# Query and scores of x's first 128 tokens in two halves of 64, all heads of the first 64 ahead

## The chip, the cores and the metric

One NeuronCore of a Trainium2 chip. It has five engines with queues of their own: TensorE (PE: matmuls, and PEld for its weight loads), VectorE (DVE), ScalarE (ACT), GpSimd (POOL) and SyncE (SP), and 16 DMA engines that move data between HBM and SBUF. The metric is the device time in microseconds, the median of three runs.

## The reference

Two blocks run one after the other on 256 tokens of width 1024, in float32. The first is a plain block (attention, a gated branch, a feed-forward of four times the width). The second has two layers; each mixes x with a context of 256 tokens and then sends every token through a table of experts. The part that matters here is that last step, cut from the reference:

```
def peer_ffn(h, w_query, sub_keys, u_tab, v_tab):        # h: 128 tokens at a time
    q = (hc @ w_query).reshape(PEER_CHUNK, PEER_HEADS, 2, D_KEY // 2)
    s = jnp.einsum('chpd,hpnd->chpn', q, sub_keys).astype(jnp.float32)
    s_top, i_top = lax.top_k(s, PEER_TOPK)
    cand = s_top[:, :, 0, :, None] + s_top[:, :, 1, None, :]
    best, pos = lax.top_k(cand.reshape(...), PEER_TOPK)
    eid = jnp.take_along_axis(cand_id, pos, axis=-1)
    gate = jax.nn.softmax(best, axis=-1).astype(hc.dtype)
    u = jnp.take(u_tab, eid, axis=0)
    act = jax.nn.gelu(jnp.einsum('chkd,cd->chk', u, hc)) * gate
    v = jnp.take(v_tab, eid, axis=0)
    return jnp.einsum('chk,chkd->cd', act, v)
```

There are 8 heads, 128 keys in each half of a head's query, and 16 best of 128 and then of the pairs. Every token so reads 128 rows of u_tab and 128 rows of v_tab, 4 KB each. In the second layer only x goes on to the output.

## The kernel before

The kernel is written as one hand-ordered program for each engine; every engine has its own copy of the same walk over the stages (mixer, routing, experts), and semaphores tie them together. Tokens are in tiles of 128: tiles 0 and 1 are the context in layer 0, 2 and 3 are x in layer 0, 4 and 5 are x in layer 1. "c0", "x0", "c1", "x1" name a layer's mixer, and `route_first` and `route_second` route its two tiles.

Routing of a tile. TensorE makes the query with `query` (L902): for each u of 0 and 1, four blocks of 128 rows (four heads), each a sum over 8 pieces of H, with weights W as the stationary side and the tile's 128 token columns as the moving side. ScalarE copies the bank to QP. `scores` (L912) multiplies QP with the keys, and ScalarE copies the banks to the tile sc. VectorE then takes `steps_of(n)`: "top" steps (`sixteen_best`, four rows of 128 scores each), "pairs" steps, and four "keys" steps. ScalarE helps twice in `routes`: at "pairs 0" it spreads the ranks (tixe, semaphore ranks_spread), and at "keys 0" it takes the exponent (best_exp). At the end TensorE transposes the expert numbers and gates (L948, L953), VectorE writes idxT and raises idx_ready (L1718 to L1721), and GpSimd may gather.

Tiles 2 and 4 (SPLIT) are routed in two parts of 64 tokens. In a part, partition 64b + t holds token t with the heads of group b, so that 64 tokens of eight heads fill 128 partitions. The first part is `routes(n, 0)` in `route_first`; the second is routed in `route_second`, beside the second tile's branch products. `query` and `scores` of such a tile are done for all 128 tokens, heads 0 to 3 first (u = 0) and heads 4 to 7 then (u = 1); the scores are written by 64 tokens (L927).

The expert stream. A visit is the work for one pair of tokens: TensorE spreads the hidden rows (L468), VectorE takes the dot with the gathered rows of u (L1174), ScalarE the gelu, and TensorE later sums the rows of v (L482). GpSimd issues four indirect DMAs for a pair (L2448, L2458), at most three pairs ahead. Visits are dealt into the rest of the program by `beat(key, us)`: each call adds its weight in us to a debt, and each 6.8 (PACE) of debt places a visit, in TensorE's program and in the same place of the others', as long as pairs are routed. Before c1 the first stream (tiles 0 to 3) is closed, and the second stream (tiles 4 and 5) is opened after `route_first("x1")`, so nothing is visited while tile 4's first part is routed. In x0 the stream of the context's tiles runs on.

What stands behind the scores in `route_first` of x0 and x1: the transposes of the hidden rows (`hidden`, L885), a gate product of the tile's second half (`merge_unit(tag, 1, "z", 0)`, L669), the routing steps with a second gate product at "pairs 0", and the transposes of the indices. Weights come in chunks of up to 2 MB through a ring of three slots; SyncE asks for the next chunk when `done_with_weights` tells that a slot's chunk has been used.

## Time and profile before

| what | us |
|---|---|
| median of three runs | 3284.21 |
| the three runs | 3279.72, 3284.21, 3287.22 |
| the profiled execution, its own time | 3281.02 |
| its span, first to last instruction | 3279.3 |
| PE busy, matmuls (share of the span) | 2348.2 (72%) |
| PE weight loads | 1356.8 (41%) |
| DVE busy | 1692.5 (52%) |
| ACT busy | 577.9 (18%) |
| POOL busy | 1481.8 (45%) |
| moved by DMA | 1097.74 MB, mean 335 GB/s |

The span is shorter than the profiled execution's time by 1.7 us, which lie around it. A busy share is a mean over stages with different limits; where one engine waits for another is read from the single instructions. The trace holds two records for one float32 matmul of the program, and as many weight loads. The page gives the granted clock of TensorE in tenths of full speed, the windows as a fraction: 1.00 is 2.4 GHz and 0.50 is 1.2 GHz.

### The profile page before, as it was taken

The numbers are of one execution on the slowest core, as the hardware profiler recorded it, in microseconds if no ns is written. First come the engines' busy times: TensorE is split into PE (matmuls) and PEld (weight loads), VectorE is DVE, ScalarE is ACT, GpSimd is POOL, SyncE is SP. The second block draws the span as 40 slices with busy tenths as digits, with TensorE's granted clock in tenths as the row PEclk, the third lists the DMA queues.
The fourth block names the chain that finished last, engine by engine and source line by source line (L and its number), as shares of the span: only waits on it lengthen the run. The fifth ranks groups of instructions, "written<-read, shape, count | busy, mean of one in ns | idle before, by whom it ended". The sixth has DMA issues, their size and how long they took to land.

```text
span 3279.3 us, 40034 instructions
## 1 busy us (share of the span) xinstructions
PE 2348.2 (72%) x13944; PEld 1356.8 (41%) x13944; DVE 1692.5 (52%) x4471; ACT 577.9 (18%) x1213; POOL 1481.8 (45%) x1577
## 2 busy tenths in 40 slices
PE   6899957899899888885775754445997765544444
PEld 5477724466676554762540300002587452100000
DVE  2521576554333577347559554443724647744444
ACT  2320231411100235111111400001331111100000
POOL 1100035444444444434547577773000556777775
PEclk9999978799999897996875755556898886555555
DMA  8958579899999986997999999995245999999998
GB/s 310 356 185 297 204 265 349 318 355 361 368 364 370 349 320 240 372 398 282 402 395 397 350 403 409 409 409 215 73 161 199 366 402 360 393 409 409 409 409 348
DMA packets 351015, 1097.74 MB, mean 335 GB/s; under 512 B 27936, under 2 KB 39264, under 8 KB 350816
## 3 DMA queue, kind: packets, MB, share of 16 engines
q0 software_dynamic: 240192, 880.90, 69.9%
q1 hardware_dynamic: 110624, 214.29, 18.2%
q8 instruction: 112, 1.84, 0.2%
q14 instruction: 87, 0.71, 0.1%
HBM read 1094.03 MB, written 1.05 MB: 334 GB/s over the span
## 4 chain that ended last, share of the span: by engine, by line
PE 44%; DVE 18%; DMA 14%; issue 12%; PEld 6%; ACT 3%; POOL 1%; PEldq 1%; DVEq 0%; ACTq 0%; POOLq 0%
PE ps L446 18%; PE ps L482 11%; DVE UV L1174 8%; DMA UV<-in_v_tab,idxT 8%; PE ps L468 4%; PE ps L669 3%; PEld ps L669 3%; DMA W<-in_w_out 3%; PEld ps L446 3%; ACT arena L1894 2%; PE ps L438 2%; DMA W<-in_w_mod 2%; DMA W<-in_w_in 1%; PE ps L613 1%; PE ps L571 1%
## 5 line engine op out<-in xcount | busy, mean ns | idle before, releaser
L1174 DVE SCALAR_TENSOR_TENSOR UV<-ps,UV 128x1024 f32<-128x1024 f32 x768 | 909.8, 1222 | 816.3 <-PE ps L468 798.6
L2448 POOL DMA_INDIRECT UV<-in_u_tab,idxT x768 | 723.8, 942 | 1156.5 <-DVE UV L1174 613.3
L482 PE MATMUL ps<-UV,acts 128*32 128x512 f32 x3072 | 607.1, 873 | 486.5 <-DVE acts L1183 341.2
L2458 POOL DMA_INDIRECT UV<-in_v_tab,idxT x768 | 725.6, 945 | 266.7 <-issue 200.9
L446 PE MATMUL ps<-H,W 128*128 128x256 f32 (+2 forms) x2528 | 503.2, 361 | 32.4 <-ACT H L1894 25.9
L446 PEld LDWEIGHTS ps<-H,W 128*128 128x128 f32 (+1 forms) x2528 | 435.3, 199 | 117.6 <-issue 66.2
L468 PE MATMUL ps<-hs,selb 32*128 32x512 bf16 x1536 | 203.1, 515 | 200.8 <-DVE UV L1174 194.3
L482 PEld LDWEIGHTS ps<-UV,acts 128*32 128x32 f32 x3072 | 76.4, 127 | 634.9 <-DVE acts L1183 436.1
L468 PEld LDWEIGHTS ps<-hs,selb 32*128 32x128 bf16 x1536 | 42.0, 96 | 595.5 <-issue 329.1
L1894 ACT ACTIVATE gel<-dots 128x2 f32<-128x2 f32 x384 | 77.2, 202 | 1152.9 <-DVE UV L1174 1141.4
L446 PE MATMUL ps<-arena,W 128*128 128x256 f32 (+1 forms) x1120 | 254.3, 384 | 11.8 <-issue 4.8
L1894 ACT ACTIVATE arena<-ps 128x512 f32<-128x512 f32 (+6 forms) x260 | 138.9, 539 | 678.1 <-PE ps L446 461.0
L446 PEld LDWEIGHTS ps<-arena,W 128*128 128x128 f32 (+1 forms) x1120 | 208.2, 189 | 68.0 <-issue 36.4
L669 PEld LDWEIGHTS ps<-H,W 128*128 128x128 f32 x1536 | 184.2, 202 | 25.3 <-issue 17.1
L669 PE MATMUL ps<-H,W 128*128 128x128 f32 x1536 | 187.7, 286 | 8.7 <-DMA W<-in_w_in 6.9
L2424 POOL DMA_DIRECT2D UV<-in_w_mod x18 | 16.1, 900 | 234.3 <-ACTq L1946 201.1
L1894 ACT ACT_TABLE_LOAD x85 | 109.1, 1283 | 54.2 <-PE ps L613 24.6
L669 PE MATMUL ps<-arena,W 128*128 128x128 f32 x640 | 84.2, 297 | 16.5 <-DMA W<-in_w_out 10.1
L669 PEld LDWEIGHTS ps<-arena,W 128*128 128x128 f32 x640 | 81.4, 211 | 24.0 <-issue 15.6
L571 PE MATMUL ps<-UV,gateT 128*32 128x512 f32 x432 | 71.4, 632 | 19.0 <-DMA W<-in_w_mod 9.4
L1462 DVE SCALAR_TENSOR_TENSOR arena<-arena,vec 128x256 f32<-128x256 f32 x180 | 79.3, 483 | 4.8 <-DVE arena L1155 0.7
L1183 DVE TENSOR_TENSOR acts<-gel,gateT 128x2 f32<-128x2 f32 x384 | 61.4, 160 | 10.4 <-ACT gel L1894 9.7
(228 smaller groups left out, 1948.5 us busy)
## 6 DMA issues: line engine op xcount, KB each, us to landing
W<-in_w_in SPq DMA_DIRECT2D x42, 2048.0 KB, 14.3
UV<-in_w_mod POOLq DMA_DIRECT2D x18, 2048.0 KB, 12.4
W<-in_w_ff SPq DMA_DIRECT2D x16, 2048.0 KB, 14.2
W<-in_w_out SPq DMA_DIRECT2D x12, 2048.0 KB, 13.9
W<-in_w_query SPq DMA_DIRECT2D x10, 2048.0 KB, 19.5
UV<-in_w_ada POOLq DMA_DIRECT2D x9, 2048.0 KB, 11.8
W<-in_w_mod POOLq DMA_DIRECT2D x6, 2048.0 KB, 20.1
UV<-in_u_tab,idxT POOLq DMA_INDIRECT x768, 8.1
```

The costliest lines, as they stand in the source:

```text
L438: last = mm(o, lhs[k], rhs[k], start=(k == 0), stop=(k == n - 1))
L446: last = mm(o, w[:, k, col:col + m], src[:, k, c], start=(k == 0), stop=(k == kt - 1))
L468: last = mm(ps[:, HB + r, :], selb[q, u:u + 1].to_broadcast([32, P]), hs[q, n % 2, s, :], start=True, stop=True)
L482: last = mm(ps[q:q + GROUP, YB, :], acts[:, tok % SLOTS, GROUP - 1 - r:2 * GROUP - 1 - r], Vs[:, tok % SLOTS, hf * 512:(hf + 1) * 512], st ...
L571: last = mm(o[q:q + 32, :], cond32[:, 4 * kh + kk, :], w[j][:, 4 * kh + kk, :], start=(kk == 0), stop=(kk == 3))
L669: last = mm(o[:, e * P:(e + 1) * P], w[:, k, e * P:(e + 1) * P], src[:, k, :], start=(k == 0), stop=(k == kt - 1))
L1174: dve.scalar_tensor_tensor(out=Us[:, j, :], in0=ps[:, b:b + 2, :].rearrange("p a b -> p (a b)"), scalar=1.0, in1=Us[:, j, :], op0=MUL, op1 ...
L1183: dve.tensor_tensor(out=acts[:, j:j + 2, GROUP - 1], in0=gel[:, j:j + 2], in1=gateT[:, n % 2, t:t + 2], op=MUL).then_inc(sem("acts"), 1)
L1462: last = dve.scalar_tensor_tensor(out=a, in0=u, scalar=wt, in1=a, op0=MUL, op1=ADD)
L1894: return act.activation(o, i, f, **kw)
L2448: pool.indirect_dma_start(Us[:, j, :], None, A["u_tab"], off).then_inc(sem(f"u_arrived{j}"), 16)
L2458: pool.indirect_dma_start(Vs[:, j, :], None, A["v_tab"], off).then_inc(sem(f"v_arrived{j}"), 16)
```

## The change

For x's first tile of each layer (tiles 2 and 4), query and scores go through four steps instead of two. The order is: first 64 tokens with heads 0 to 3, first 64 tokens with heads 4 to 7, then the same for the other 64 tokens. The new functions `query_half` and `scores_half` stand in TensorE's and ScalarE's programs; the weights of both u are kept in the ring until the second half has used them. Two branches of `scores` for a tile of two parts are gone. The waits count by `queries_before(n)`, and VectorE's first "top" steps wait for the scores of their own 64 tokens. The debt of the beats is 4.0 for each of the four query steps, 16 in all, where two queries and two score steps had 18. The context's first tile is untouched.

```diff
+            def query_half(tag, n, u, r, first=False):
+
+                w = weights(("wq", tag, n % 2, u))
+                o, at = bank(("wq", n, u, r)), n % 2 * P + HALF * r
+                for e in range(4):
+                    last = feature(o[:, e * HALF:(e + 1) * HALF], w, e * P, H, DT, first=first and e == 0, c=slice(at, at + HALF))
+                full(last, ("wq", n, u, r))
+                if r:
+                    done_with_weights()
+
+            def scores_half(n, u, r):
+
+                pe.wait_ge(sem("query_ready"), queries_before(n) + 2 * r + u + 1)
+                o = [bank(("sc", n, u, r, p)) for p in range(2)]
+                for i in range(2):
+                    for b in range(2):
+                        h, at = 4 * u + 2 * b + i, HALF * r
+                        for p in range(2):
+                            last = mm(o[p][HALF * b:HALF * b + HALF, i * P:(i + 1) * P], QP[n % 2][64 * p:64 * p + 64, h, at:at + HALF],
+                                      keys[64 * p:64 * p + 64, h, :], start=True, stop=True)
+                            if (i, b) == (1, 1):
+                                full(last, ("sc", n, u, r, p))
...
                 n = TILE_OF[tag]
-                for u in range(2):
+                for u in range(2 if tag == "c0" else 0):
                     query(tag, n, u, first=(u == 0))
                     beat(("wq", n, u), 7.0)
                     if u == 0:
                         pe.wait_ge(sem("keys_loaded"), nxt("keys_loaded", 16))
                     scores(n, u)
+                for i in range(4 if tag != "c0" else 0):
+                    r, u = i // 2, i % 2
+                    query_half(tag, n, u, r, first=(i == 0))
+                    beat(("wq", n, u, r), 4.0)
+                    if i == 0:
+                        pe.wait_ge(sem("keys_loaded"), nxt("keys_loaded", 16))
+                    scores_half(n, u, r)
...
-                    dve.wait_ge(sem("scores_ready"), 4 * n + 2 * (e // 2 + 1 if parts(n) == 1 else e + 1))
+                    dve.wait_ge(sem("scores_ready"), 2 * queries_before(n) + 2 * (e // 2 + 1 if parts(n) == 1 else 2 * r + e + 1))
...
+            def query_half(n, u, r):
+
+                p = full_bank(act, ("wq", n, u, r))
+                link(A_(QP[n % 2][:, 4 * u:4 * u + 4, HALF * r:HALF * r + HALF], p[:, 0:4 * HALF].rearrange("p (e t) -> p e t", e=4)))
+                act.sem_inc(free(("wq", n, u, r)), 1)
+                act.sem_inc(sem("query_ready"), 1)
+                beat("wq", n, u, r)
+
+            def scores_half(n, u, r):
+
+                for q in range(2):
+                    p = full_bank(act, ("sc", n, u, r, q))
+                    link(A_(s4[:, r, 2 * u:2 * u + 2, q, :], p[:, 0:2 * P].rearrange("p (h k) -> p h k", h=2)))
+                    act.sem_inc(free(("sc", n, u, r, q)), 1)
+                    act.sem_inc(sem("scores_ready"), 1)
```

TensorE in layer 1, `route_first("x1")`, before. L446 is the query (here one row for 32 matmuls, 128 columns moving), L927 the scores, L885 the transposes of the hidden rows, L669 the two gate products, L953 and L954 the transposes of the indices:

```order
L446 MATMUL ps<-H,W 128x128 x32
L927 MATMUL ps<-arena 64x128 x16
L446 MATMUL ps<-H,W 128x128 x32
L927 MATMUL ps<-arena 64x128 x16
L885 MATMUL ps<-ident,H 128x128 x8
L669 MATMUL ps<-H,W 128x128 x64
L953 MATMUL ps<-ident,arena 64x64
```

The same place in the changed kernel, where L450 is the query, L924 the scores, L889, L673 and L972 the rest:

```order
L450 MATMUL ps<-H,W 128x64 x32
L924 MATMUL ps<-arena 64x128 x8
L450 MATMUL ps<-H,W 128x64 x32
L924 MATMUL ps<-arena 64x128 x8
L450 MATMUL ps<-H,W 128x64 x32
L924 MATMUL ps<-arena 64x128 x8
L450 MATMUL ps<-H,W 128x64 x32
L924 MATMUL ps<-arena 64x128 x8
L889 MATMUL ps<-ident,H 128x128 x8
L673 MATMUL ps<-H,W 128x128 x64
L972 MATMUL ps<-ident,arena 64x64
```

Two groups of 32 query matmuls have become four, all ahead of the transposes and the gate products.

ScalarE at the same place, before, from the first query copy to the exponent. The row that waits for `ranked` is the spread of the ranks:

```order
L1894 ACTIVATE arena<-ps 128x512 [waits psum_full,idx_ready]
L1894 ACTIVATE arena<-ps 128x2x2x128 [waits act_chain,psum_full] x2
L1894 ACTIVATE arena<-ps 128x512 [waits act_chain,psum_full]
L1894 ACTIVATE arena<-ps 128x2x2x128 [waits act_chain,psum_full] x2
L1894 ACTIVATE arena<-ps 128x512 [waits act_chain,psum_full]
L1894 ACTIVATE arena<-ps 128x512 [waits psum_full]
L1894 ACT_TABLE_LOAD [waits psum_full]
L1894 ACTIVATE VC<-ps 128x512 [waits gates_used]
L1894 ACTIVATE arena<-arena 128x2048 [waits act_chain,ranked]
```

And in the changed kernel:

```order
L1922 ACTIVATE arena<-ps 128x4x64 [waits psum_full,idx_ready]
L1922 ACTIVATE arena<-ps 128x2x128 [waits act_chain,psum_full] x2
L1922 ACTIVATE arena<-ps 128x4x64 [waits act_chain,psum_full]
L1922 ACTIVATE arena<-ps 128x2x128 [waits act_chain,psum_full] x2
L1922 ACTIVATE arena<-ps 128x4x64 [waits act_chain,psum_full]
L1922 ACTIVATE arena<-ps 128x2x128 [waits act_chain,psum_full] x2
L1922 ACTIVATE arena<-ps 128x4x64 [waits act_chain,psum_full]
L1922 ACTIVATE arena<-ps 128x2x128 [waits act_chain,psum_full] x2
L1922 ACTIVATE arena<-ps 128x512 [waits act_chain,psum_full]
L1922 ACTIVATE arena<-ps 128x512 [waits psum_full]
L1922 ACT_TABLE_LOAD [waits psum_full]
L1922 ACTIVATE VC<-ps 128x512 [waits gates_used]
```

The copies of the second 64 tokens now stand ahead of the gate product's copy (VC) and of the spread behind it, whose row reads as before.

TensorE in layer 0, `route_first("x0")`, of the changed kernel, from the first query step to the gate product. A pair of rows L472 and L486 is a visit:

```order
L450 MATMUL ps<-H,W 128x64 x32
L924 MATMUL ps<-arena 64x128 x8
L450 MATMUL ps<-H,W 128x64 x32
L472 MATMUL ps<-hs,selb 128x512 x4
L486 MATMUL ps<-UV,acts 32x512 x4
L924 MATMUL ps<-arena 64x128 x8
L450 MATMUL ps<-H,W 128x64 x32
L472 MATMUL ps<-hs,selb 128x512 x4
L486 MATMUL ps<-UV,acts 32x512 x4
L924 MATMUL ps<-arena 64x128 x8
L450 MATMUL ps<-H,W 128x64 x32
L924 MATMUL ps<-arena 64x128 x8
```

Two visits stand between the four query steps and a third behind the transposes that follow; before there were also three up to the gate product, one behind each query and one behind the transposes.

## Rows read from the trace of the kernel before

**Rows 1.** Windows: stretch, its length, busy us, granted clock, DMA share, GB/s.

```profile
core 0: us, PE busy (x) PEld busy (x) DVE busy (x) ACT busy (x) POOL busy (x), PEclk, DMA share, GB/s
...
1490.00:1520.00 30.00, 13.99 (x100) 10.27 (x104) 25.80 (x112) 6.54 (x7) 6.87 (x7) 0.67 0.40 143
...
2252.00:2541.00 289.00, 240.51 (x1612) 197.72 (x1608) 130.59 (x365) 83.63 (x150) 1.87 (x2) 0.91 0.38 129
...
2550.00:2710.00 160.00, 118.05 (x936) 83.71 (x938) 86.40 (x235) 23.05 (x50) 81.18 (x86) 0.83 1.02 393
...
2860.00:3240.00 380.00, 184.94 (x892) 26.64 (x892) 183.19 (x384) 16.03 (x76) 278.10 (x298) 0.50 1.03 409
...
1520.00:1780.00 260.00, 170.79 (x1248) 99.53 (x1240) 168.54 (x552) 37.73 (x80) 146.84 (x156) 0.74 1.02 393
```

**Rows 2.** Timeline of GpSimd: start, us, instruction, count [idle before <- releaser].

```profile
1513.38 0.94 POOL L2448 DMA_INDIRECT UV<-in_u_tab,idxT  x1 [21.61 <-DVEq L1721]
...
2541.64 0.94 POOL L2448 DMA_INDIRECT UV<-in_u_tab,idxT  x1 [286.48 <-DVEq L1721]
```

**Rows 3.** Timeline of TensorE's matmuls in layer 1, `route_first("x1")`.

```profile
2495.10 10.20 PE L446 MATMUL ps<-H,W 128*128 128x128 f32 x64 [3.98 <-ACT H L1894]
...
2506.20 1.10 PE L927 MATMUL ps<-arena 64*64 64x128 f32 x32 [0.91 <-ACTq L2240]
2507.23 7.41 PE L446 MATMUL ps<-H,W 128*128 128x128 f32 x64
2515.45 1.10 PE L927 MATMUL ps<-arena 64*64 64x128 f32 x32 [0.80 <-ACTq L2240]
...
2517.41 7.31 PE L669 MATMUL ps<-H,W 128*128 128x128 f32 x64
2524.98 7.38 PE L669 MATMUL ps<-H,W 128*128 128x128 f32 x64 [0.26 <-issue]
2539.54 0.49 PE L953 MATMUL ps<-ident,arena 64*64 64x64 f32 x4 [7.18 <-DVEq L1708]
```

**Rows 4.** Timeline there of VectorE (top 1, keys 0) and ScalarE (the spread).

```profile
2518.20 0.88 DVE L1612 MAX8 arena<-arena 128x8 f32<-128x128 f32 x4 [4.02 <-ACTq L2252]
...
2526.88 1.91 ACT L1894 ACTIVATE arena<-arena 128x2048 bf16<-128x2048 bf16 x1 [0.18 <-ACT VC L1894]
...
2532.97 0.69 DVE L1630 TENSOR_TENSOR arena<-arena,iotax 128x1024 bf16<-128x1024 bf16 x1
```

**Rows 5.** Timeline of TensorE and VectorE in layer 0, `route_first("x0")`.

```profile
1438.62 9.31 PE L446 MATMUL ps<-H,W 128*128 128x128 f32 x64 [2.54 <-ACT H L1894]
...
1458.07 0.40 PE L468 MATMUL ps<-hs,selb 32*128 32x512 bf16 x4
1458.39 1.07 PE L482 MATMUL ps<-UV,acts 128*32 128x512 f32 x8
...
1470.67 0.40 PE L468 MATMUL ps<-hs,selb 32*128 32x512 bf16 x4
...
1473.55 0.87 DVE L1612 MAX8 arena<-arena 128x8 f32<-128x128 f32 x4
...
1481.88 1.94 PE L482 MATMUL ps<-UV,acts 128*32 128x512 f32 x8
```

**Rows 6.** Records by line: ns min/median/max, first and last start; one timeline row.

```profile
L446 PE MATMUL ps<-H,W x29: 274/276/276, 2501.8 to 2504.9; 128*128 128x128 f32 x29
L446 PEld LDWEIGHTS ps<-H,W x28: 191/192/193, 2501.9 to 2504.9; 128*128 128x128 f32 x28
...
L446 PE MATMUL ps<-H,W x23: 420/422/422, 2495.7 to 2500.3; 128*128 128x128 f32 x23
L446 PEld LDWEIGHTS ps<-H,W x22: 333/333/334, 2495.9 to 2500.4; 128*128 128x128 f32 x22
...
2346.99 0.97 PEld L825 LDWEIGHTS ps<-onecol,arena 96*128 96x128 f32 x8 [0.53 <-issue]
```

**Rows 7.** Windows: stretch, its length, busy us, granted clock, DMA share, GB/s.

```profile
2352.00:2366.00 14.00, 14.00 (x25) 6.27 (x25) 11.99 (x22) 0.93 (x2) 0.00 (x0) 0.50 0.01 1
2491.00:2501.00 10.00, 6.02 (x29) 5.93 (x29) 3.55 (x9) 3.49 (x9) 0.00 (x0) 0.50 0.35 135
```

More of the change, by code:

```diff
@@ L46, in part_no, with queries_before @@
     return sum(parts(m) for m in range(n)) + r
+def queries_before(n):
+    return sum(2 * parts(m) for m in range(n))
 def steps_of(n):
@@ L912, in scores @@
             def scores(n, a):
-                pe.wait_ge(sem("query_ready"), 4 * (n // 2) + 2 * (n % 2) + a + 1)
+                pe.wait_ge(sem("query_ready"), queries_before(n) + a + 1)
                 o = [bank(("sc", n, a, p)) for p in range(2)]
-                for hh in range(4 if parts(n) == 1 else 0):
+                for hh in range(4):
                     h = 4 * a + hh
@@ L922, in scores @@
                             full(last, ("sc", n, a, p))
-                for i in range(4 if parts(n) == 2 else 0):
-                    for b in range(2):
-                        h, at = 4 * a + 2 * b + i % 2, i // 2 * HALF
-                        for p in range(2):
-                            last = mm(o[p][HALF * b:HALF * b + HALF, i * P:(i + 1) * P], QP[n % 2][64 * p:64 * p + 64, h, at:at + HALF],
-                                      keys[64 * p:64 * p + 64, h, :], start=True, stop=True)
-                            if (i, b) == (3, 1):
-                                full(last, ("sc", n, a, p))
                 beat(("sc", n, a), 2.0)
@@ L1736, in route_first @@
                 n = TILE_OF[tag]
-                for u in range(2):
+                for u in range(2 if tag == "c0" else 0):
                     beat("wq", n, u)
                     beat("sc", n, u)
+                for i in range(4 if tag != "c0" else 0):
+                    beat("wq", n, i % 2, i // 2)
                 for u in range(2 if tag == "c0" else 0):
@@ L2246, in scores @@
                     p = full_bank(act, ("sc", n, a, q))
-                    if parts(n) == 1:
-                        link(A_(w4[:, 4 * a:4 * a + 4, q, :], p.rearrange("p (a b) -> p a b", b=P)))
-                    else:
-                        link(A_(s4[:, :, 2 * a:2 * a + 2, q, :], p.rearrange("p (r h k) -> p r h k", r=2, h=2)))
+                    link(A_(w4[:, 4 * a:4 * a + 4, q, :], p.rearrange("p (a b) -> p a b", b=P)))
                     act.sem_inc(free(("sc", n, a, q)), 1)
@@ L2277, in route_first @@
                     act.wait_ge(sem("idx_ready"), part_no(n, 0))
-                for u in range(2):
+                for u in range(2 if tag == "c0" else 0):
                     query(n, u)
                     scores(n, u)
+                for i in range(4 if tag != "c0" else 0):
+                    query_half(n, i % 2, i // 2)
+                    scores_half(n, i % 2, i // 2)
                 mods_at(tag, "queried")
```

## Prediction

> **What bounds the kernel now.** I read the busy shares and DMA of chosen stretches first, then the waits of the GpSimd queue, then single instructions around the two places that the change touches. Over each of the long stretches 1520 to 1780, 2550 to 2710 and 2860 to 3240 us the DMA engines are full (share 1.02, 1.02, 1.03) [rows 1]. They carry the gathers of expert rows, four indirect DMAs for a pair of tokens. So the end comes a fixed amount of traffic after the moment at which gathers may begin, as long as nothing later starves them. Twice they have nothing to do. In 1490 to 1520 the share is 0.40, and in 2252 to 2541 it is 0.38 [rows 1]. Both holes end when the indices of x's first 64 tokens come out of routing: at 1513.38 after 21.61 us of waiting and at 2541.64 after 286.48 us the first gather of such a half is issued, released by VectorE at L1721 [rows 2]. I call these moments G0 (layer 0) and G1 (layer 1). A microsecond later at either is a microsecond later at the end, and both add up: the hardware works in program order behind them, on full DMA.
>
> What sets G1 [rows 3, 4]: TensorE makes query 0 at 2495.10, its scores at 2506.20, query 1 at 2507.23, scores at 2515.45, some transposes, then two gate products at 2517.41 and 2524.98. VectorE starts the second "top" step at 2518.20, having waited for the scores. It works without a stop to the "keys" step at 2532.97, and the transposes of the indices follow at 2539.54, for which TensorE had waited 7.18 us. ScalarE's spread of the ranks (2526.88, 1.91 us, done at 2528.8), which the keys step needs, stands behind ScalarE's copy of the first gate product. It has 4.2 us to spare.
>
> What sets G0 [rows 5]: here experts of the context's tokens are worked on in between. TensorE starts query 0 at 1438.62; after queries, scores, transposes, three such visits and the first gate product comes the visit at 1470.67, 32.05 us later. VectorE has that visit ahead of its first top step, which begins at 1473.55. There is no slack: what TensorE does before 1470.67 is on the path.
>
> **What the change removes and adds.** Two passes over the query weights for 128 tokens become four for 64. Each pass still has 32 matmuls, which the trace shows as 64 records, and 64 loads of 128x128 weights; only the moving side falls from 128 to 64 columns. The sum thus hangs on the price of a record with 64 columns, which the trace doesn't have. From both sides: with 128 columns at the high clock 29 records start from 2501.8 to 2504.9, 111 ns apart. With one moving column, eight loads of 128 columns take 0.97 us; less the last one's 0.19 that is 111 ns apart as well [rows 6]. One column costs as much as 128, so the load sets the pace and 64 columns lie between equal ends: 7.4 us for a half pass, as for a whole one (2507.23). At the low clock 23 records of 128 columns start from 2495.7 to 2500.3, 209 ns apart. The load's own duration grows there from 192 to 333 ns, the matmul's from 276 to 422, by nearly the same amount [rows 6]. I take it that loads go slower with the clock and price a half pass at 64 x 0.209 = 13.4 us.
>
> The Trainium skill, TensorE: Matmul & The Clock Gate, section LDWEIGHTS, gives a load as its columns over 1.2, so about 107 ns, with no word of the clock. By it a half pass at the low clock would be 6.8 us and the whole sum would be that of the second case below. The rows [rows 6] speak against it: 333 ns against 192.
>
> **Which clock.** Both first passes begin after TensorE has been idle for some microseconds. In 2491 to 2501 the granted clock is 0.50, the 1.2 GHz level [rows 7], and it rose during the first whole pass, which streams its columns without a gap. A half pass has loads that take as long and half the columns. The nearest stretches are 2860 to 3240, busy about half the time, at 0.50 for 380 us [rows 1], and 2352 to 2366, busy 14.00 of 14.00 us with narrow weights, also at 0.50 [rows 7]. I take the low level to last through all four half passes of layer 1. In layer 0 the visits and scores between the passes are dense work, which may lift it midway.
>
> Layer 1 at the low clock: four passes 53.5; each followed by a wait for the copy (0.9) and a score group of half size (0.5, at the low clock 1.0), 7.6 together; the transposes 1.9; the gate product 7.3 and 1.0 for the part of it still slow. From 2495.1 that ends at 2566.4 instead of 2524.7, 41.7 later. Less the spread's 4.2: G1 **+37.5**. At the high clock: passes 10.2 + 3 x 7.4 = 32.4, then 4 x 1.4, 1.0 and 7.3, 16.7 later, G1 +12.5.
>
> Layer 0: at the high clock passes 9.3 + 3 x 7.4 = 31.5, three visits of 1.4 (1458.07 to 1459.46) [rows 5], score groups 2.0, two waits of 0.9 that no visit covers, transposes 1.0, the gate product 7.4: 47.9 instead of 32.05, G0 +15.9. At the low clock throughout: 53.5 + 3 x 2.5 (the low clock's 1.94 [rows 5] and twice 0.32 ahead of it) + 4.0 + 1.8 + 2.0 + 8.2 = 77, G0 +45. Between the ends I take **+30**, the level rising at the visit after the second or third pass.
>
> Side costs at nothing: the first half's scores come a little earlier, but the spread or the visit ends later, so VectorE waits. The weight ring gives query 0's slot back after the third pass instead of the first. The weights of the second gate product are then asked for 22 us or more before they are needed at the low clock, and about 18 at the high one; SyncE's queue otherwise keeps its order. ScalarE's eight score copies are half as wide as the four before. Should that cover fail, one 2 MB chunk costs up to the 14.3 us in which such chunks land (median of the page). From G0 and G1 on, the order is the old one.
>
> Sum: 37.5 + 30 = 67.5 us. The profiled execution took 3281.0, so 3348.5; the median of the three runs is 3284.2, 3.2 above it, so **3352**.
>
> **Rivals.**
> Second case, the clock is high in nearly all passes, or loads don't slow with it: +12.5 and +15.9 = 28.4, 3312.6. For it: before, the first pass of layer 0 took 9.31 us against 10.20 in layer 1 [rows 3, 5], so less of it ran at the low level. Against it: a half pass streams columns half of the time.
>
> Third case, the other side: columns, not loads, price a record, 0.056 us, so a half pass is 3.6 us and the first one, paced by ScalarE, some 6.6, together 17.4. Layer 0: 17.4 + 4.2 + 2.0 + 1.8 + 1.0 + 7.4 = 33.8, G0 +1.8. Layer 1: the first gate product ends 1.7 later, the spread at 2530.5, which is 2.4 ahead of the old keys step, and VectorE, with its scores by 2510, is there before: G1 -2.4. Together -0.6, 3283.6, not slower. It decides below 4.5 us for a half pass, 70 ns a record. The eight one-column records [rows 6] speak against it. The Trainium skill, TensorE: Matmul & The Clock Gate, section Back-to-back issue gap, gives 1 to 64 columns some 60 cycles and 128 columns 134, which is this case.
>
> Fourth, the delay is partly taken up later: between G0 and the end of the first stream a stretch with the DMA not quite full could catch up some microseconds. That moves the first two cases down by up to 8 us and is in the range.
>
> **How the numbers follow.** Low clock for most of the half passes 0.70 (layer 0 from +16 to +45, so 3334 to 3370 as its own range), second case 0.17, third 0.08, something else 0.05. A measurement tells 0.2%, 6.6 us, from no change. The first two cases are slower, with a little of the rest: slower 0.90, same 0.07, faster 0.03. The range must reach into the second case: 3306 (3312.6 less 6 caught up) to 3370 (+82.5 and the spread of the runs, 3).
>
> **What would show it.** Records with 64 columns 111 ns apart at the high and about 209 at the low clock; a granted clock of 0.50 from the first half pass of layer 1 to the gate product; the first gather of that half at 2541.6 + G0's shift + 37; the keys step released by ScalarE's spread; a longer hole in the DMA at both places and the same full DMA behind. Records 56 to 70 ns apart would make it wrong, and so would an end that moves less than the two first gathers.

## The result and the profile after

The changed kernel takes 3357.64 us, the median of six runs (3345.56 to 3365.09); the kernel before, measured beside it, 3282.76 (3273.68 to 3289.12). The ratio is 1.0231, with a 95% interval of 1.0211 to 1.0251: slower by 2.3%. The forecast was 3352 with a range of 3306 to 3370. The profiled execution is the shortest of the six, 3345.56 us; what probably makes the others longer comes below, with x0_only.

The head of the page of the changed kernel:

```profile
span 3343.8 us, 40590 instructions
...
PE 2418.5 (72%) x14200; PEld 1418.9 (42%) x14200; DVE 1692.1 (51%) x4471; ACT 580.0 (17%) x1225; POOL 1486.5 (44%) x1577
```

TensorE has 70 us more of busy time and the span is 64.5 longer; VectorE, ScalarE and GpSimd have nearly the busy time that they had. The first gathers of the two first halves, from the timeline of GpSimd (start, us, instruction, idle time before and what ended it), answer to [rows 2]:

```profile
1540.28 0.94 POOL L2492 DMA_INDIRECT UV<-in_u_tab,idxT  x1 [22.81 <-DVEq L1747]
...
2606.64 0.94 POOL L2492 DMA_INDIRECT UV<-in_u_tab,idxT  x1 [325.98 <-DVEq L1747]
```

They moved from 1513.38 to 1540.28 and from 2541.64 to 2606.64, by 26.9 and 65.0 us, the second including the first. The end moved by 64.5. From here on I call the time from a layer's first query record to this gather its **stretch**. Before, the stretches were 74.76 us in layer 0 (from 1438.62) and 46.54 in layer 1 (from 2495.10); now they are 102.94 and 85.59, that is 28.18 and 39.05 more. Between the first gather and the next layer's first record lie 980.8 us (981.7 before), behind the second gather 737.2 (737.7): hardly a microsecond was given back.

TensorE's matmuls in layer 1, the same columns as [rows 3] (L450 is the query, L924 the scores, L889 the transposes of hidden rows, L673 the gate products, L972 the transposes of the indices):

```profile
2521.05 13.89 PE L450 MATMUL ps<-H,W 128*128 128x64 f32 x64 [3.98 <-ACT H L1922]
2535.64 1.13 PE L924 MATMUL ps<-arena 64*64 64x128 f32 x16 [0.69 <-issue]
2536.70 13.91 PE L450 MATMUL ps<-H,W 128*128 128x64 f32 x64
...
2552.26 13.91 PE L450 MATMUL ps<-H,W 128*128 128x64 f32 x64
...
2567.83 13.91 PE L450 MATMUL ps<-H,W 128*128 128x64 f32 x64
...
2585.16 8.88 PE L673 MATMUL ps<-H,W 128*128 128x128 f32 x64
2594.30 7.38 PE L673 MATMUL ps<-H,W 128*128 128x128 f32 x64 [0.26 <-issue]
2604.79 0.34 PE L972 MATMUL ps<-ident,arena 64*64 64x64 f32 x4 [3.11 <-DVEq L1734]
```

Four half passes of 13.9 us stand where two whole ones of 10.20 and 7.41 stood. Windows of the changed kernel (stretch, length, busy us, granted clock, DMA share, GB/s, as in [rows 1, 7]):

```profile
2536.70:2550.60 13.90, 13.90 (x68) 13.72 (x64) 5.17 (x32) 0.77 (x2) 0.00 (x0) 0.50 0.01 1
...
2567.80:2581.80 14.00, 13.94 (x68) 13.72 (x64) 0.46 (x2) 0.79 (x3) 0.00 (x0) 0.50 0.39 145
...
2252.00:2606.00 354.00, 293.77 (x1792) 238.41 (x1792) 142.50 (x390) 85.82 (x161) 16.82 (x18) 0.81 0.38 135
...
2925.00:3305.00 380.00, 185.10 (x896) 26.39 (x888) 183.00 (x382) 15.81 (x75) 279.55 (x298) 0.50 1.03 409
```

The half passes ran at 0.50, the 1.2 GHz level, until the gate product. The window of the hole in the DMA, 2252 to the first gather, has the same share of 0.38 as the 289 us before, but here it takes in the last gathers of the first stream (16.82 us of GpSimd instead of 1.87). The hole itself grew by 39.5 us, which is what GpSimd's wait for the indices grew by (325.98 instead of 286.48). The last stream behind it is as full as before (1.03).

What held VectorE, and ScalarE's spread of the ranks, as in [rows 4]:

```profile
2553.56 0.87 DVE L1638 MAX8 arena<-arena 128x8 f32<-128x128 f32 x4 [10.34 <-ACTq L2285]
...
2598.22 0.69 DVE L1656 TENSOR_TENSOR arena<-arena,iotax 128x1024 bf16<-128x1024 bf16 x1 [29.93 <-ACT arena L1922]
...
2596.20 1.91 ACT L1922 ACTIVATE arena<-arena 128x2048 bf16<-128x2048 bf16 x1 [0.18 <-ACT VC L1922]
```

VectorE had the scores of the first 64 tokens at 2553.5, was through with the top and pairs steps at 2568.3, and then waited 29.93 us for the spread, which stands on ScalarE behind the copy of the gate product, which stands on TensorE behind the two half passes of the other 64 tokens. Being first ahead of the others brought VectorE nothing.

Layer 0, as in [rows 5] (L472 and L486 are a visit):

```profile
1437.34 13.70 PE L450 MATMUL ps<-H,W 128*128 128x64 f32 x64 [2.55 <-ACT H L1922]
...
1452.79 13.91 PE L450 MATMUL ps<-H,W 128*128 128x64 f32 x64
1466.64 0.61 PE L472 MATMUL ps<-hs,selb 32*128 32x512 bf16 x4
1467.18 1.88 PE L486 MATMUL ps<-UV,acts 128*32 128x512 f32 x8
1468.99 0.67 PE L924 MATMUL ps<-arena 64*64 64x128 f32 x16
1469.59 7.36 PE L450 MATMUL ps<-H,W 128*128 128x64 f32 x64
...
1478.98 7.36 PE L450 MATMUL ps<-H,W 128*128 128x64 f32 x64
...
1497.56 0.40 PE L472 MATMUL ps<-hs,selb 32*128 32x512 bf16 x4
```

Two half passes at the low clock, 13.70 and 13.91 us, and from the visit between the second and the third on two at the high one, 7.36 each. The visit behind the gate product came 60.22 us after the first record instead of 32.05; from it to the gather it took 42.7 us in both kernels.

### The profile page after: what moved, and what is told of

Same layout as the page of the kernel before. It is cut to its first block, busy times and chain, and to the rows that moved or that the text cites. A ratio compares the mean times of both kernels' runs of the same rounds, so it can differ in the third digit from the quotient of the medians.

```text
span 3343.8 us, 40590 instructions
## 1 busy us (share of the span) xinstructions
PE 2418.5 (72%) x14200; PEld 1418.9 (42%) x14200; DVE 1692.1 (51%) x4471; ACT 580.0 (17%) x1225; POOL 1486.5 (44%) x1577
## 3 DMA queue, kind: packets, MB, share of 16 engines
q8 instruction: 114, 1.87, 0.2%
## 4 chain that ended last, share of the span: by engine, by line
PE 46%; DVE 17%; DMA 13%; issue 12%; PEld 6%; ACT 3%; POOL 2%; PEldq 1%; DVEq 0%; ACTq 0%; POOLq 0%
PE ps L450 19%; PE ps L486 11%; DMA UV<-in_v_tab,idxT 8%; DVE UV L1200 7%; PE ps L673 4%; PE ps L472 3%; PEld ps L450 3%; PEld ps L673 2%; ACT arena L1922 2%; PE ps L442 2%; DMA W<-in_w_mod 2%; DMA W<-in_w_in 1%; DMA W<-in_w_out 1%; PE ps L575 1%; PE ps L617 1%
## 5 line engine op out<-in xcount | busy, mean ns | idle before, releaser
L486 PE MATMUL ps<-UV,acts 128*32 128x512 f32 x3072 | 610.4, 878 | 487.6 <-DVE acts L1209 349.1
L450 PE MATMUL ps<-H,W 128*128 128x256 f32 (+3 forms) x2784 | 564.3, 369 | 31.9 <-ACT H L1922 25.1
L450 PEld LDWEIGHTS ps<-H,W 128*128 128x128 f32 (+1 forms) x2784 | 495.4, 214 | 118.2 <-issue 66.4
L472 PE MATMUL ps<-hs,selb 32*128 32x512 bf16 x1536 | 203.1, 515 | 203.1 <-DVE UV L1200 197.0
L486 PEld LDWEIGHTS ps<-UV,acts 128*32 128x32 f32 x3072 | 76.5, 127 | 636.6 <-DVE acts L1209 442.8
L472 PEld LDWEIGHTS ps<-hs,selb 32*128 32x128 bf16 x1536 | 41.7, 96 | 597.8 <-issue 329.1
L450 PE MATMUL ps<-arena,W 128*128 128x256 f32 (+1 forms) x1120 | 254.3, 384 | 11.7 <-issue 4.7
L450 PEld LDWEIGHTS ps<-arena,W 128*128 128x128 f32 (+1 forms) x1120 | 207.7, 189 | 68.3 <-issue 36.3
L673 PEld LDWEIGHTS ps<-H,W 128*128 128x128 f32 x1536 | 188.3, 205 | 22.4 <-issue 16.3
L673 PE MATMUL ps<-H,W 128*128 128x128 f32 x1536 | 191.8, 289 | 5.8 <-DMA W<-in_w_in 4.2
L2468 POOL DMA_DIRECT2D UV<-in_w_mod x18 | 16.1, 900 | 235.1 <-ACTq L1974 201.2
L673 PE MATMUL ps<-arena,W 128*128 128x128 f32 x640 | 82.6, 293 | 13.0 <-DMA W<-in_w_out 6.9
L673 PEld LDWEIGHTS ps<-arena,W 128*128 128x128 f32 x640 | 79.8, 207 | 20.3 <-issue 16.8
```

The lines of the kernel that those rows point to most:

```text
L450: last = mm(o, w[:, k, col:col + m], src[:, k, c], start=(k == 0), stop=(k == kt - 1))
L472: last = mm(ps[:, HB + r, :], selb[q, u:u + 1].to_broadcast([32, P]), hs[q, n % 2, s, :], start=True, stop=True)
L486: last = mm(ps[q:q + GROUP, YB, :], acts[:, tok % SLOTS, GROUP - 1 - r:2 * GROUP - 1 - r], Vs[:, tok % SLOTS, hf * 512:(hf + 1) * 512], st ...
L673: last = mm(o[:, e * P:(e + 1) * P], w[:, k, e * P:(e + 1) * P], src[:, k, :], start=(k == 0), stop=(k == kt - 1))
```

## The experiments

The kernel before was timed beside each group of experiments: 3280.1 us beside x1_only to wide_moving, 3281.0 beside warm to spread_first, 3279.3 beside warm14 and narrow_load, 3280.2 beside the last two. The stretches are first record to first gather, each from one profiled execution; passes are those of layer 1.

| kernel | layer 0 stretch | layer 1 stretch | query passes, layer 1 | median us | ratio to before, 95% interval |
|---|---|---|---|---|---|
| before | 74.76 | 46.54 | 10.20, 7.41 | 3282.8 | 1 |
| the change | 102.94 | 85.59 | 13.89, 3 x 13.91 | 3357.6 | 1.0211 to 1.0251 |
| x1_only | 74.91 | 84.74 | 13.74, 3 x 13.91 | 3319.3 | 1.0097 to 1.0132 |
| x0_only | 119.68 | 46.54 | 10.20, 7.41 | 3319.0 | 1.0082 to 1.0129 |
| umajor | 119.91 | 84.93 | 13.70, 3 x 13.91 | 3363.2 | 1.0219 to 1.0270 |
| wide_moving | 90.85 | 58.15 | 10.21, 3 x 7.41 | 3310.8 | 1.0068 to 1.0106 |
| warm | 103.25 | 84.15 | 12.88, 3 x 13.91 | 3339.1 | 1.0153 to 1.0189 |
| before_warm | 73.86 | 44.89 | 8.54, 7.41 | 3278.1 | 0.9983 to 1.0004 |
| late | 74.70 | 61.79 | 13.88, 13.91, 7.26, 7.36 | 3302.8 | 1.0053 to 1.0084 |
| spread_first | 103.28 | 83.68 | 13.70, 3 x 13.91 | 3352.4, one run | none |
| warm14 | 88.43 | 55.27 | 7.25, 3 x 7.36 | 3305.5 | 1.0058 to 1.0100 |
| narrow_load | 87.71 | 54.70 | 9.73, 6.42, 6.43, 6.42 | 3302.0 | 1.0056 to 1.0097 |
| before_split | 82.42 | 53.87 | 13.41, 11.53 | 3297.6 | 1.0033 to 1.0063 |
| late_narrow | 74.47 | 45.02 | 10.50, 6.43, 6.43, 6.42 | 3286.6 | 1.0010 to 1.0028 |

In warm, before_warm and warm14 the stretch begins with the first real query record, behind the extra matmuls.

### One layer alone: x1_only and x0_only

Both keep the two functions of the change for one tile and give the other the whole passes back:

```diff
+HALVED = (4,)          # x0_only: (2,)
 def queries_before(n):
-    return sum(2 * parts(m) for m in range(n))
+    return sum(4 if m in HALVED else 2 for m in range(n))
...
-                for i in range(4 if tag != "c0" else 0):
+                for i in range(4 if n in HALVED else 0):
```

> Only layer 1 (tile 4) goes in four half passes; layer 0 (tile 2) has its two whole passes back. My theory: the two places are independent and add up, each delaying its own first gather. In the traces the stretch from the first query to the first gather grew by 39.05 us in layer 1 (46.54 to 85.59) and by 28.18 in layer 0 (74.76 to 102.94). Expected here: 46.5 + 39 = 85.6 us in layer 1, 74.8 in layer 0, and a time of 3282.8 + 39 = 3322 us (3318 to 3326). Rival, a delay in layer 0 is partly caught up later and layer 1 costs more than its own share: over 3330.

> Only layer 0 (tile 2) goes in four half passes; layer 1 is as before. Theory (independent, additive): from the first query to the first gather 102.9 us in layer 0 and 46.5 in layer 1, time 3282.8 + 28 = 3311 us (3306 to 3315). Rival, the stream of layer 0 has room and takes part of the delay up before the mixer of layer 1: below 3304.

Layer 1 came as expected: 3319.3 us, 39.2 above the kernel before, runs within 2 us of each other (3318.0 to 3319.7). The two medians add up to 78.1, near the 74.9 of the change. Layer 0 did not come as expected: 38.9 above instead of 28, and the runs lie from 3310.2 to 3326.9. The windows of TensorE in layer 0 of x0_only, at the second half pass, the visit behind it and the third half pass, and below them those of the changed kernel, tell why:

```profile
1456.30:1470.20 13.90, 13.90 (x72) 13.78 (x68) 0.00 (x0) 0.77 (x2) 0.00 (x0) 0.50 0.01 1
1470.20:1473.60 3.40, 3.40 (x29) 0.99 (x28) 2.45 (x5) 0.59 (x2) 0.67 (x1) 0.50 0.00 0
1473.60:1487.60 14.00, 13.94 (x68) 13.73 (x64) 0.00 (x0) 0.79 (x3) 3.07 (x4) 0.50 0.44 150
```

```profile
1452.80:1466.60 13.80, 13.80 (x68) 13.72 (x64) 0.00 (x0) 0.77 (x2) 0.00 (x0) 0.50 0.00 1
1466.60:1469.60 3.00, 3.00 (x30) 0.75 (x29) 2.23 (x3) 0.59 (x2) 0.19 (x1) 0.62 0.00 0
1469.60:1477.00 7.40, 7.35 (x68) 7.21 (x64) 0.22 (x3) 0.78 (x3) 3.56 (x4) 1.00 0.73 247
```

The instructions are the same, and the clock rose in one execution and not in the other. So layer 0 has two outcomes from one execution to the next: about 103 us (the change, warm, spread_first) where it rises midway, and about 120 (x0_only, umajor) where it stays low through all four. That is two values of one stretch over five profiles. x0_only's own profile is of its longest run, 3326.9, 46.8 above the kernel before, and its shortest, 3310.2, is 30.1 above it: about the delays of the one and of the other outcome. The times alone don't prove it, since the kernel before also spreads by 8 to 15 us, and of the change itself only the shortest run has a profile.

### The order: umajor

```diff
-                    r, u = i // 2, i % 2
+                    u, r = i // 2, i % 2
```

(and the waits and ScalarE's copies to match)

> All four half passes stay, at the same place, but in the order of before: heads 0 to 3 for the first and then the second 64 tokens, then heads 4 to 7. Theory: the cost lies in the number and the clock of the passes, not in whose scores come first, because VectorE waits for the spread behind all four. Expected: the same as the changed kernel, 3357.6 us within 4, both stretches within 2 us of 85.6 and 102.9. Rival, the order itself costs (VectorE's early first steps or the ring slots held longer): nearer to the kernel before, below 3340.

Measured 3363.2 us, a little more than the 3357.6 expected and far from 3340. The layer-1 stretch is 84.93: whose scores come first doesn't matter, four passes do. Layer 0 took its long outcome in this profile (119.91 instead of 102.9), which is the miss of this expectation.

### Twice the columns: wide_moving

```diff
-    last = feature(o[:, e * HALF:(e + 1) * HALF], w, e * P, H, DT, first=first and e == 0, c=slice(at, at + HALF))
+    last = feature(o[:, e * P:(e + 1) * P], w, e * P, H, DT, first=first and e == 0, c=in_h(n))
```

> The changed kernel, but each of the four passes streams all 128 token columns, and ScalarE copies the 64 that the step wants; the other 64 are computed and dropped, so TensorE has twice the columns to do. Theory: a record is paced by its weight load, and the half pass is slow because the low clock lasts; with 128 columns the clock rises in the first pass and each later pass takes 7.4 us. Expected: passes 10.2, 7.4, 7.4, 7.4 in layer 1, granted clock 1.00 after the first, the layer-1 stretch 46.5 + 12.5 = 59 us, the layer-0 one 74.8 + 16 = 91, time 3282.8 + 28.4 = 3311 us (3305 to 3318), 46 faster than the changed kernel. Rival, columns or the traffic of the passes set the price: as slow as the changed kernel or slower, 3358 or more.

The passes of layer 1 in the timeline of TensorE:

```profile
2510.03 10.21 PE L450 MATMUL ps<-H,W 128*128 128x128 f32 x64 [3.98 <-ACT H L1922]
...
2521.53 7.41 PE L450 MATMUL ps<-H,W 128*128 128x128 f32 x64
```

Twice the columns, 47 us faster: 3310.8, the two stretches 16.1 and 11.6 above the kernel before, where the prediction's second case had 15.9 and 12.5. So the change costs some 28 us by its additional passes even at the high clock (31 by the medians), and the rest, 44 to 47, by the low one.

### What lowers the clock: warm and warm14

```diff
                 o, at = bank(("wq", n, u, r)), n % 2 * P + HALF * r
+                for _ in range(6 if first else 0):          # warm14: 14
+                    mm(o[:, 0:SEQ], ones[:, :], wide(dftc[:, :, :]), start=True, stop=True)
```

> The changed kernel with six extra matmuls (ones times a constant table, 128x128 by 256 columns, result overwritten) on TensorE ahead of the first half pass of both layers, where it waits 2.5 and 4.0 us for H. Theory: the half passes are slow because they begin at the low clock and cannot raise it; once it is high they keep it, as the last two of layer 0 did (1.00, 7.36 us each). Expected: four passes of 7.4 us at a granted clock of 1.00 in both layers, stretches from the first record to the first gather of 59 us in layer 1 and 91 in layer 0 plus 1 to 2 for the extra work, time 3282 + 30 + 3 = 3315 us (3310 to 3322). Rival, 64 columns cannot hold the high level without visits in between: only the first pass or two gain, 3335 to 3350.

Measured 3339.1, within the rival's numbers, and my theory in this form fell. (The two stretches of the profile are only 1.1 us shorter in sum than those of the change, while the medians are 18.5 apart. Where these come from is not shown; more runs with the short outcome of layer 0 are a possibility.) Windows around the start of the first half pass of layer 1 (2521.24):

```profile
2520.00:2521.00 1.00, 0.00 (x0) 0.00 (x0) 0.97 (x4) 0.30 (x1) 0.00 (x0) 1.00 0.78 283
2521.00:2522.00 1.00, 0.76 (x4) 0.59 (x4) 0.61 (x2) 1.00 (x4) 0.00 (x0) 1.00 0.00 0
...
2524.00:2525.00 1.00, 1.00 (x9) 1.00 (x9) 0.00 (x0) 0.00 (x0) 0.00 (x0) 0.90 0.00 0
2525.00:2526.00 1.00, 1.00 (x6) 1.00 (x6) 0.00 (x0) 0.00 (x0) 0.00 (x0) 0.50 0.00 0
```

The pass began at the high clock and lost it within 4 us. That leaves two readings: half passes lose the level by themselves, or the start does, where TensorE first waits 1.30 us for H and then 15 records take 3.02 us because ScalarE delivers H piece by piece.

> As warm, with 14 extra matmuls instead of six. With six the granted clock was 1.00 when the first half pass of layer 1 began (2521.24) and fell to 0.50 at about 2524.9, after a wait of 1.30 us for H and 15 records in 3.02 us, each waiting for ScalarE's pieces of H. Theory: not the half passes themselves lose the level but their ragged start; in late the level held through two half passes in a row (7.26 and 7.36 us). Fourteen take about 6.4 us (12 records took 2.76), so that all pieces of H are there when the pass begins, some 2.6 us later than before. Expected: four passes of 7.4 us in both layers, granted clock 1.00, the first gather 58 to 60 us after H came in layer 1 and about 91 to 93 in layer 0, time 3281 + 30 = 3311 us (3306 to 3318). Rival, half passes lose the level sooner or later by themselves: 3325 to 3345.

```profile
2509.75 7.25 PE L450 MATMUL ps<-H,W 128*128 128x64 f32 x64
...
2526.84 7.36 PE L450 MATMUL ps<-H,W 128*128 128x64 f32 x64
2535.39 7.36 PE L450 MATMUL ps<-H,W 128*128 128x64 f32 x64
...
2539.00:2543.00 4.00, 3.75 (x34) 3.61 (x33) 3.41 (x18) 0.21 (x1) 0.00 (x0) 1.00 0.63 238
```

Half passes don't lose the level by themselves. With a gap-free start all four ran at 1.00 in both layers (the last row is the end of the fourth), for 33 us in layer 1, and the kernel takes 3305.5, 52 less than the change, for 28 additional matmuls whose products nobody reads. These delay the first real record by 1.9 us in layer 1 and 3.5 in layer 0, which the stretches of the table leave out; from ScalarE's first piece of H the first gather comes after 57.8 and 92.6 us, as expected. The 14 matmuls do two things at once, they take the wait away and keep TensorE at work longer ahead of the pass, and no run separates the two. So half passes held the level over this time, but from the low one they did not win it back in layer 1 of the change, and the low clock is some 50 of the 75 us.

### The clock in the kernel before: before_warm

The same six matmuls ahead of its first whole pass of tiles 2 and 4.

> The kernel before with the same six extra matmuls ahead of the first whole query pass of tiles 2 and 4. Theory: whole passes raise the clock by themselves after some 5 us, so there is only 10.20 - 7.41 = 2.8 us to win in layer 1 and 9.31 - 7.41 = 1.9 in layer 0, less what the extra work overhangs (about 1 each): 3280.1 - 3 = 3277 us, 0.1%, within what can be told. Rival, the extra work delays more than it gives: 3283 or more.

```profile
2489.39 8.54 PE L446 MATMUL ps<-H,W 128*128 128x128 f32 x64 [1.30 <-ACT H L1896]
...
2494.00:2496.00 2.00, 2.00 (x21) 2.00 (x20) 0.00 (x0) 0.00 (x0) 0.00 (x0) 1.00 0.03 8
```

This adds to the reading of warm: behind the same six matmuls, the same wait of 1.30 us for H and the same pieces of H from ScalarE, a whole pass kept the level (the row is from its middle), where the half pass had fallen to 0.50. In layer 0 it was the same, 8.37 against 11.85 us. So the start alone doesn't lose the level; in warm it was such a start together with 64 moving columns behind 128-column loads.

The interval of the ratio, 0.9983 to 1.0004, includes no change. In the profile the passes took 8.54 instead of 10.20 in layer 1 and 8.37 instead of 9.31 in layer 0; the stretches are 1.65 and 0.90 shorter. It is the best version of this study by its median, and not one that the measurement separates from the kernel before.

### What stands behind: spread_first and late

In spread_first ScalarE spreads the ranks ahead of its copy of gate product 0, in layer 1:

```diff
                 if tag != "c0":
+                    if n == 4:
+                        spread_ranks(PH // 2, part_no(n, 0) + 1, 0)
                     merge_unit(tag, 1, "z", 0)
```

> The changed kernel, but in layer 1 ScalarE spreads the ranks ahead of its copy of gate product 0. Theory: VectorE's keys step then starts some 10 us earlier (it had waited 29.93 us for the spread), but the transposes of the indices stand on TensorE behind both gate products, which end 80.6 us after the first query record. So only the 3.1 us go that TensorE had waited there: the layer-1 stretch falls from 85.6 to 82.5 us. Rival, the spread alone was the path: 75.5 us. (Layer 0 is untouched; only the layer-1 stretch is read.)

The stretch fell by 1.9 us instead of 3.1, and 0.9 of these are not the edit's: the passes and the two gate products took 79.8 us from the first record instead of 80.6. VectorE's row shows the next wait in line:

```profile
2593.88 0.69 DVE L1656 TENSOR_TENSOR arena<-arena,iotax 128x1024 bf16<-128x1024 bf16 x1 [19.61 <-ACT arena L1922]
...
2608.24 0.22 DVE L1731 TENSOR_REDUCE arena<-arena 128x4 f32<-128x64 f32 x1 [8.62 <-ACT arena L1922]
```

The keys step starts some 10 us sooner relative to the first record, as both theories had it, but then VectorE waits 8.62 us for ScalarE's exponent, which stands behind the copy of gate product 1. I had overlooked that copy. Each wait was covered by one behind it, and all of them stand behind TensorE's four passes.

In late (layer 0 as before) the second half's passes go behind gate product 0, beside the pairs step, and gate product 1 behind the first gather:

```diff
+                if n in HALVED:
+                    halves(0)
...
-                    routes(n, 0, {"pairs 0": [lambda: merge_unit(tag, 1, "z", 1)]})
+                    routes(n, 0, {"pairs 0": [lambda: halves(1) if n in HALVED else merge_unit(tag, 1, "z", 1)]})
...
+                    if tag == "x1":
+                        later["top 0"].insert(0, lambda: merge_unit(tag, 1, "z", 1))
```

> Layer 0 as in the kernel before. In layer 1 the first 64 tokens take their two half passes, then the transposes and gate product 0, and only then, beside the first pairs step, the two half passes of the other 64; gate product 1 moves behind the first gather. Theory: what delays the first gather are the passes ahead of it on TensorE at the low clock. With the second two at the high clock behind gate product 0 they end 59 us after the start of the first, and the first gather comes at about 61 us (where all four ahead gave 84.7 and the kernel before 46.5): time 3280.1 + 14.5 = 3295 us (3290 to 3303). If the clock falls again in the second two: 73 us, 3307. Rival, that VectorE's chain behind the scores of the second 64 or the weight ring sets the time: as x1_only, 3319.

```profile
2526.44 1.97 PE L893 MATMUL ps<-ident,H 128*128 128x128 f32 x8
2528.20 7.71 PE L676 MATMUL ps<-H,W 128*128 128x128 f32 x64
2535.74 7.26 PE L453 MATMUL ps<-H,W 128*128 128x64 f32 x64
...
2544.18 7.36 PE L453 MATMUL ps<-H,W 128*128 128x64 f32 x64
```

The clock rises in the gate product (0.50 ahead of it, 1.00 at its end), and the half passes behind it keep it. The stretch is 61.79 us (61 expected). The time is 3302.8, 8 more than expected: from the gather to the end it took 743.2 us instead of 737.7. Gate product 1 now lies in that part; that it is the cause was not tested.

### What a record costs: narrow_load and before_split

narrow_load splits each matmul of the half passes in two with 64 weight columns each, the same products:

```diff
-    last = feature(o[:, e * HALF:(e + 1) * HALF], w, e * P, H, DT, first=first and e == 0, c=slice(at, at + HALF))
+    for b in range(2):
+        last = feature(o[HALF * b:HALF * b + HALF, e * HALF:(e + 1) * HALF], w, e * P + HALF * b, H, DT, m=HALF,
+                       first=first and e + b == 0, c=slice(at, at + HALF))
```

> The changed kernel, but each query matmul is split in two with 64 weight columns each (the same products, into the two halves of the partitions): 128 records with loads of 128x64 in a half pass instead of 64 with 128x128, the moving side 64 columns as before. Theory: a record is paced by its load, whose time goes by its columns; a load of 64 columns should take about half (some 105 ns at the low clock, 55 at the high), so a pass still takes 13.4 to 14 us at the low clock and 7.4 at the high one and the time stays at 3357 us (3345 to 3367). Rival, each record has a fixed price whatever is loaded: passes of 27 us at the low clock, layer 1 alone 54 us later, 3440 or more.

```profile
2504.17 9.73 PE L450 MATMUL ps<-H,W 128*64 128x64 f32 x128 [3.98 <-ACT H L1924]
...
2515.19 6.42 PE L450 MATMUL ps<-H,W 128*64 128x64 f32 x128
```

Its windows, the end of the first pass and the second:

```profile
2508.00:2514.00 6.00, 5.90 (x103) 5.76 (x102) 0.00 (x0) 0.00 (x1) 0.00 (x0) 0.82 0.01 3
2515.20:2521.60 6.40, 6.40 (x132) 6.28 (x128) 5.06 (x32) 0.77 (x2) 0.00 (x0) 1.00 0.01 3
```

The largest miss: 3302.0 us, not 3357. With 64 columns moving, records do go by their loads at the high clock, 50 ns (6.42 / 128) where a 128-column load gives 115 (7.36 / 64). But the clock rose during the first pass, although busy TensorE looked the same (full in both). I had priced the records and left the clock where it was. Most of the gain is the clock's: wide_moving, which also had the high one but records of 116 ns, took 3310.8 us, 8.8 more.

before_split gives the kernel before the same split, with all 128 columns moving:

> The kernel before, with each query matmul of tiles 2 and 4 split in two with 64 weight columns each, and all 128 token columns moving: 128 records with 128x64 loads and 128 columns in a whole pass. In narrow_load a record with a 64-column load and 64 moving columns took 50 ns (6.42 us for 128), and in the other runs one with a 128-column load took 111 to 116 ns whether 64 or 128 columns moved. Theory: a record costs the larger of its two sides, some 0.8 ns per column, load or moving. Then 128 moving columns cost about 104 ns even with the narrow load and a pass takes 128 x 0.104 = 13.3 us instead of 7.4, two passes about 11 us more in each layer, time 3280 + 22 = 3302 us (3297 to 3306). Rival, only the load sets the price: 6.4 to 7.4 us a pass, as the kernel before or 3 us faster.

```profile
2515.37 11.53 PE L446 MATMUL ps<-H,W 128*64 128x128 f32 x128
```

90 ns a record (11.53 / 128) against 50 with 64 columns moving and the same load: with the narrow load it is the moving side that counts. The pass was 11.5 us rather than 13.3, so a moving column costs less than a loaded one (0.70 against 0.90 ns), and the time 3297.6 rather than 3302. The four prices at the high clock, each a pass divided by its records, loaded columns by moving columns: 128 by 128, 116 ns; 128 by 64, 115; 64 by 128, 90; 64 by 64, 50. A whole pass with its 128-column loads is at its load's price, and halving its moving side gives nothing.

The Trainium skill, TensorE: Matmul & The Clock Gate, section LDWEIGHTS, gives a load as its columns over 1.2: 107 and 53 ns. At the high clock, with 64 columns moving, the pace of the records comes near it (115 and 50 ns); at the low clock a half pass of 13.91 us is 217 ns a record, twice the figure of the Trainium skill.

### The pieces together: late_narrow

late, with the split loads, and with the last half pass moved behind ScalarE's exponent:

```diff
+                    routes(n, 0, {"pairs 0": [lambda: second(0) if n in HALVED else merge_unit(tag, 1, "z", 1)],
+                                  "keys 0": [lambda: second(1)]})
```

> Layer 0 as before. Layer 1 as late, with the split loads of narrow_load, and the last half pass with its scores moved behind ScalarE's exponent, which in late had stood behind the score copies (VectorE waited 6.12 us for it). Theory: passes of 9.7, 6.4, 6.4 and 6.4 us at a high clock; the scores of the first 64 tokens are ready some 19 us after the first record (21.4 before), the transposes of the indices follow the last scores at about 43.5, the first gather comes at about 45.5 us, where the kernel before has 46.5. Behind it late lost 5.5 us more than the kernel before did between the first gather and the end, which I expect again: 3280 - 1 + 5 = 3284 us (3278 to 3290). Rival, the chain is bound by TensorE's queue more than this: 3290 or more; or the loss behind the gather was an accident: 3277 to 3280.

```profile
2516.12 0.87 DVE L1664 MAX8 arena<-arena 128x8 f32<-128x128 f32 x4 [2.39 <-ACTq L2320]
...
2538.61 0.34 PE L986 MATMUL ps<-ident,arena 64*64 64x64 f32 x4 [0.32 <-issue]
```

VectorE gets the scores of the first 64 tokens sooner, 20.7 us after the first record instead of 23.1, and the transposes of the indices follow TensorE's last scores with 0.32 us between. The stretch is 45.02 us (45.5 expected), 1.5 shorter than in the kernel before, the only one of the kernels with half passes in which it is. The time, 3286.6, is still 0.2% above the kernel before: from the gather to the end it took 741.6 us, 3.9 more. I expected 3284.

## Why the prediction was right, point by point

**The path.** Right. Both first gathers moved, both movements are in the end (26.9, then 65.0, then 64.5), and the long streams are as full as before.

**The price of a half pass.** Right at both levels: 7.36 us at the high clock (7.4 forecast) and 13.91 at the low (13.4). The third case, columns alone setting the price, needed 70 ns a record or less at the high clock, and the runs showed 115. Columns do count where the load is narrow: with 64-column loads a record took 90 ns with 128 columns moving and 50 with 64. The table of the Trainium skill that the prediction names for this case (TensorE: Matmul & The Clock Gate, section Back-to-back issue gap) is given there for single matmuls; for a stream of loads and matmuls the same section says that both set the spacing, and these prices agree.

**Layer 1.** +39.05 against +37.5. The passes gave 55.6 us (53.5 forecast), the waits and scores 6.7 (7.6 forecast), and the first gate product took 8.88 instead of 8.3. Its end moved by 43.4 relative to the first record (41.7 forecast). Less the slack of the spread, 4.1 (4.2 forecast), that is the 39.

**Layer 0.** +28.18 against +30 in the profiled execution, with the level rising at the visit after the second pass, as assumed. But here one number stood for two cases. The two ends of the range, +16 and +45, were both measured (wide_moving 16.1, x0_only 44.9), and the changed kernel itself seems to go from one run to another between +28 and some +45 (the one profile of it has +28, and two relatives with the same four passes have +45). The step "between the ends I take +30" treated as one unknown value what is two outcomes of the same program. No row behind the point told how often the level would rise, so that the profile came within 2 us of +30 is luck. The two outcomes fit the median, 3357.6, which lies 5.6 above the forecast, while the profiled execution, 3345.6, lies 2.9 below 3348.5: four of the six runs are 3355 or more. The medians of all runs are 74.9 us apart, where the sum had 67.5.

**Side costs at nothing.** Right for the order and the ring as far as tested: umajor, which gives the first slot back after two half passes, has the same layer-1 stretch (84.93).

**The clock.** The level was right, on thin ground. The two stretches that I took for the nearest are not like a half pass: weight loads take 26.64 of 380 us in the one and 6.27 of 14 in the other [rows 1, 7], and 13.72 of 13.90 in a half pass. The cause was incomplete too. I argued from the half pass's few columns alone. wide_moving and narrow_load bear it out as far as rising goes: with 128 columns, or with narrower loads between the 64, the level rose in the first pass. But warm14 and late's last two passes show that half passes keep the high level once they have it and begin in full; in warm it went with a start that waited for H.

**No catching up.** The fourth case, up to 8 us taken up later, found next to nothing: 980.8 and 737.2 us behind the two gathers, where the kernel before has 981.7 and 737.7.

## What to carry to other kernels

Halving the moving side of a matmul whose weight load is as wide as the array doubles the passes and saves nothing on each: see first which of the two sides sets the spacing of the records, and if the tile must shrink, shrink the load with it. An order that serves some tokens first helps only if the work of the others goes behind the step that frees the path; here it still stood ahead of it on TensorE. And cost every matmul stage at both clocks, and ask which one it will get in the order that it will have, with the waits at its start: here that was some 50 of 75 us, and in one place it differed from one execution to another.

## What the runs showed of the hardware

- At the high clock a float32 record with a 128-column load took 115 to 116 ns whether 64 or 128 columns moved; with a 64-column load 50 and 90 ns. At the low clock 128 by 64 took 217 ns, and the load's own duration was 333 ns instead of 192, so the load slows with the clock.
- TensorE, busy but for gaps of 0.6 to 0.7 us, stayed at 1.2 GHz for more than 60 us (four half passes of layer 1, from 2521 to 2584), and in narrow_load, with the same products to make, and in wide_moving, with twice the columns, it went to 2.4 GHz within the first pass. The busy share doesn't tell the two apart; the granted clock does.
- Half passes kept the 2.4 GHz level for 33 us where they began with it and without a wait (warm14), and lost it within 4 us where the first had to wait for its input (warm); after the same wait a whole pass kept it (before_warm).
- At the same visit behind the same half pass the clock rose in one execution and not in another (1.00 against 0.50 in the next pass), worth 17 us. What decides it is not in the rows that I read, and stays open.
